# Six PSUM banks for the latent block's tiles, sums of squares two tiles behind the products, inverse roots in place in two alternating places

## The reference, cut to what matters

```python
h = _rmsnorm(h_res, norm_w[l])
proj = h @ w_in[l]
q_lat, kv_lat, k_pe, g_mla, na_q, na_k, na_v, g_na = jnp.split(proj, split_at, axis=-1)
...
q = (_rmsnorm(q_lat, q_lat_w) @ w_uq).reshape(B, L, MLA_HEADS, MLA_NOPE + MLA_ROPE)
kv = (_rmsnorm(kv_lat, kv_lat_w) @ w_ukv).reshape(B, L, MLA_HEADS, MLA_NOPE + MLA_V)
q_nope, q_pe = q[..., :MLA_NOPE], q[..., MLA_NOPE:]
k_nope, v = kv[..., :MLA_NOPE], kv[..., MLA_NOPE:]
q_nope = _rmsnorm(q_nope, qn_w)
k_nope = _rmsnorm(k_nope, kn_w)
...
q_pe = _rope(_rmsnorm(q_pe, qpe_w), cos[None, :, None, :], sin[None, :, None, :])
```

## Time and profile before

| | us |
|---|---|
| median of 3 runs | 1271.04 |
| lowest and highest run | 1270.48, 1272.4 |
| profiled execution | 1273.77 |
| its span in the trace | 1272.1 |
| mean granted TensorE clock | 0.989 |
| latent block on TensorE, first tile to first score matmul | 973.61 to 1060.98 |

### The profile page before, as it was taken

How to read it: one execution, slowest core, us unless ns; L and a number is a source line. 1 busy time by engine, 2 the same in 40 slices (tenths; PEclk the granted TensorE clock), 3 DMA queues, 4 the chain that set the end, 5 groups by cost and what they waited for, 6 DMA issues and landing times.

```text
span 1272.1 us, 18656 instructions
## 1 busy us (share of the span) xinstructions
PE 1195.5 (94%) x7112; PEld 987.8 (78%) x7112; DVE 703.3 (55%) x1170; ACT 544.3 (43%) x1002; POOL 86.2 (7%) x124
## 2 busy tenths in 40 slices
PE   7999999999999998898978899999989788999998
PEld 4665787787788886677955899999979775798467
DVE  3544567676533334779369554445574635455843
ACT  3234321222232223555258554445465556466742
POOL 0002011122100002000000200000000000020500
PEclk9999999999999999899999999999999999999899
DMA  8889355687522232224320345655534332374011
GB/s 304 315 299 323 130 180 164 196 284 248 189 96 100 100 99 66 66 67 133 100 67 1 100 159 174 194 177 188 160 119 145 100 100 66 61 225 138 33 47 53
DMA packets 121366, 183.32 MB, mean 144 GB/s; under 512 B 4305, under 2 KB 92672, under 8 KB 121296
## 3 DMA queue, kind: packets, MB, share of 16 engines
q1 hardware_dynamic: 113744, 154.64, 36.8%
q0 software_dynamic: 7552, 27.73, 6.9%
HBM read 181.31 MB, written 1.05 MB: 143 GB/s over the span
## 4 chain that ended last, share of the span: by engine, by line
PE 80%; DVE 10%; ACT 4%; issue 3%; POOL 1%; DMA 1%; DVEq 0%; SPq 0%; ACTq 0%; POOLq 0%
PE ps L458 19%; PE ps L459 19%; PE ps L460 19%; PE ps L774 2%; PE ps L775 2%; PE ps L776 2%; PE ps L814 2%; DVE wl L443 1%; PE ps L2038 1%; PE ps L2082 1%; ACT wh L436 1%; DVE big L885 1%; PE ps L2369 1%; PE ps L2371 1%; PE ps L2370 1%
## 5 line engine op out<-in xcount | busy, mean ns | idle before, releaser
L443 DVE TENSOR_TENSOR wl<-raw,wh 128x1024 fp32r<-128x1024 f32 (+1 forms) x246 | 296.4, 1209 | 263.3 <-ACT wh L436 260.7
L458 PE MATMUL ps<-hh,wh 128*128 128x256 f32 (+2 forms) x1256 | 420.3, 335 | 17.9 <-DVE hl L588 11.4
L459 PE MATMUL ps<-hl,wh 128*128 128x256 f32 (+2 forms) x1256 | 411.2, 327 | 0.0
L460 PE MATMUL ps<-hh,wl 128*128 128x256 f32 (+2 forms) x1256 | 410.2, 327 | 0.0
L436 ACT ACTIVATE wh<-raw 128x1024 fp32r<-128x1024 f32 (+1 forms) x246 | 252.8, 1031 | 278.1 <-PE ps L460 256.3
L458 PEld LDWEIGHTS ps<-hh,wh 128*128 128x128 f32 x1256 | 238.8, 190 | 60.6 <-issue 27.5
L460 PEld LDWEIGHTS ps<-hh,wl 128*128 128x128 f32 x1256 | 239.2, 190 | 20.9
L459 PEld LDWEIGHTS ps<-hl,wh 128*128 128x128 f32 x1256 | 238.1, 190 | 22.3 <-issue 1.9
L458 PE MATMUL ps<-ah,wh 128*128 128x256 f32 (+2 forms) x392 | 132.5, 338 | 7.4 <-DVE big L870 3.7
L459 PE MATMUL ps<-al,wh 128*128 128x256 f32 (+2 forms) x392 | 129.7, 331 | 0.0
L460 PE MATMUL ps<-ah,wl 128*128 128x256 f32 (+2 forms) x392 | 129.5, 330 | 0.0
(11 more groups left out here) (225 smaller groups left out, 1427.1 us busy)
## 6 DMA issues: line engine op xcount, KB each, us to landing
raw<-in_ffn_w_in SPq DMA_DIRECT2D x44, 1024.0 KB, 5.1
raw<-in_ffn_w_out SPq DMA_DIRECT2D x22, 1024.0 KB, 5.0
raw<-in_w_in SPq DMA_DIRECT2D x22, 1024.0 KB, 5.3
big<-in_w_ada SPq DMA_DIRECT2D x16, 1024.0 KB, 9.3
big<-in_w_ada POOLq DMA_DIRECT2D x24, 512.0 KB, 4.5
ex<-in_w_ada POOLq DMA_DIRECT2D x24, 512.0 KB, 5.2
raw<-in_diff_w_in SPq DMA_DIRECT2D x12, 1024.0 KB, 5.1
raw<-in_w_out SPq DMA_DIRECT2D x8, 1024.0 KB, 4.9
```

The costliest lines, as they stand in the source:

```text
L443: ins = nc.vector.tensor_tensor(place(wl), v, place(wh).bitcast(F32), ALU.subtract)
L458: nc.tensor.matmul(o, w_hi, m_hi, start=first, stop=False, **kw)
L459: nc.tensor.matmul(o, w_hi, m_lo, start=False, stop=False, **kw)
L460: return nc.tensor.matmul(o, w_lo, m_hi, start=False, stop=last, **kw)
```

## The change

In the latent block the tiles take the six banks 0, 1, 2, 5, 6, 7 in turn, and everything behind a head tile's products moves one tile back: the sum of squares of tile i - 2 is issued behind tile i, and so are its inverse root, its scaling (i - 2) and its turning (i - 3). In the other lists the distance stays one tile and the banks 0, 1, 2. Each list now starts at bank 0, and a tile waits for the last user of its bank, across lists. In all lists Ln and Exp work in one place, `rstd[:, h % 2]`, which alternates from head to head, so that ScalarE waits for the scaling of head h - 2 and not of h - 1.

```diff
+        last_in = {}
+        for phase in PHASES:
+            banks = (0, 1, 2, 5, 6, 7) if phase is MLA_UNITS else (0, 1, 2)
+            for i, u in enumerate(phase):
+                u["bank"] = banks[i % len(banks)]
+                u["lag"] = 2 if phase is MLA_UNITS else 1
+                u["prev"] = last_in.get(u["bank"])
+                last_in[u["bank"]] = u
...
-            bank = u["u"] % 3
+            bank = u["bank"]
...
-            if u["u"] >= 3:
-                v = ALL_UNITS[u["u"] - 3]
+            v = u["prev"]
+            if v:
...
-            for i in range(len(phase) + 1):
+            lag = phase[0]["lag"]
+            for i in range(len(phase) + lag):
...
-                if 1 <= i <= len(phase) and phase[i - 1]["kind"] == "head":
-                    u = phase[i - 1]
+                if i >= lag and phase[i - lag]["kind"] == "head":
+                    u = phase[i - lag]
...
-                    positive(act, s_unrm, u["h"])
-                    link(nc.scalar.activation(rstd[0:m, 1, 0:w], ps[0:m, 3 + u["h"] % 2, 0:w], ACT.Ln,
+                    positive(act, s_unrm, u["h"] - 1)
+                    inverse = rstd[0:m, u["h"] % 2, 0:w]
+                    link(nc.scalar.activation(inverse, ps[0:m, 3 + u["h"] % 2, 0:w], ACT.Ln,
                                               bias=eps_c[0:m, 0:1], scale=1.0 / u["dim"]))
-                    nc.scalar.activation(rstd[0:m, 0, 0:w], rstd[0:m, 1, 0:w], ACT.Exp,
-                                         scale=-0.5).then_inc(s_urs, 1)
+                    nc.scalar.activation(inverse, inverse, ACT.Exp, scale=-0.5).then_inc(s_urs, 1)
...
-                            out=dst, in0=o[:, a:b], scalar=par_of(u["gain"])[0:m, :], in1=rstd[0:m, 0, a:b],
+                            out=dst, in0=o[:, a:b], scalar=par_of(u["gain"])[0:m, :], in1=rstd[0:m, u["h"] % 2, a:b],
...
-                if i >= 2 and phase[i - 2].get("rope"):
-                    u = phase[i - 2]
+                if i > lag and phase[i - lag - 1].get("rope"):
+                    u = phase[i - lag - 1]
```

More of the change, by code:

```diff
@@ L842, in units_act @@
                         ins.then_inc(s_ucp, 1)
-                if i >= 1 and phase[i - 1]["kind"] == "head":
-                    u = phase[i - 1]
+                if i >= lag and phase[i - lag]["kind"] == "head":
+                    u = phase[i - lag]
                     m, w = u["cols"], u["w"]
                     act.wait_ge(s_usum, u["h"] + 1)
-                    positive(act, s_unrm, u["h"])
-                    link(nc.scalar.activation(rstd[0:m, 1, 0:w], ps[0:m, 3 + u["h"] % 2, 0:w], ACT.Ln,
+                    positive(act, s_unrm, u["h"] - 1)
+                    inverse = rstd[0:m, u["h"] % 2, 0:w]
+                    link(nc.scalar.activation(inverse, ps[0:m, 3 + u["h"] % 2, 0:w], ACT.Ln,
                                               bias=eps_c[0:m, 0:1], scale=1.0 / u["dim"]))
-                    nc.scalar.activation(rstd[0:m, 0, 0:w], rstd[0:m, 1, 0:w], ACT.Exp,
-                                         scale=-0.5).then_inc(s_urs, 1)
+                    nc.scalar.activation(inverse, inverse, ACT.Exp, scale=-0.5).then_inc(s_urs, 1)
                 for q in halves_after(phase, i):
@@ L855, in units_dve @@
         def units_dve(dve, link, mark, phase):
-            for i in range(len(phase) + 2):
-                if 1 <= i <= len(phase) and phase[i - 1]["kind"] == "head":
-                    u = phase[i - 1]
+            lag = phase[0]["lag"]
+            for i in range(len(phase) + lag + 1):
+                if lag <= i < len(phase) + lag and phase[i - lag]["kind"] == "head":
+                    u = phase[i - lag]
                     m = u["cols"]
```

## The result

The change makes the kernel faster: 1257.89 us (median of 4 runs, 1257.21 to 1258.08) against 1271.32 us (4 runs, 1270.48 to 1272.4) of the kernel before. The ratio is 0.9889, 95% interval 0.9874 to 0.9904, so 12.2 to 16.0 us of gain around 13.4. The forecast was 1257.5. The profiled execution took 1257.90 us, where the forecast for it was about 1260.3.

The account below looks back on a forecast made before the run. TensorE's waits in the latent block were taken as the bound: 19.4 us lost now, 6.2 then, gain 13.2 + 0.3 = 13.5 us from 1271.04, so 1257.5 us; range 1253.5 to 1261.5.

Parts of the forecast that it names:

- The 15 waits go: Latent block: with six banks TensorE's 15 waits for a VectorE scaling, 12.9 us together, go but for a remnant.
- the restart: TensorE in the latent block: each wait loses a further 0.24 or 0.16 us at its restart, 4.2 us in all.
- The split is late next: Second and third quarters' first value tiles: TensorE waits some 2.0 us for VectorE's split at each; cost 4.5 us.
- Sums that wait for a square: Key heads' quarters: two waits of 0.51 and 0.49 us stay, about 0.65 each with restart; cost 1.7 us with late banks.
- a late bank: Key heads' quarters: 0.2 us added to each of the two remaining waits of a sum for its square.
- The roots: Ln and Exp in one place on ScalarE: the wait for the previous head's scaling goes, off TensorE's path; zero gain.
- the row maximum: Start of the attention: it starts 2.53 us behind the first score matmul; rounding and split come earlier, gain 0.3 us.
- The clock: Latent block: one low-clock fall, 1.5 us of work lost, stays; none or two widen the range 1.5 us each side.
- ScalarE's queue takes the banks' part: Latent block: sums wait for squares at about eight rounding places, giving back some 7 us, 1264.5 us; chance 0.10.
- Slower: Latent block: squares' two places and sums' two banks expose the whole chain at 20 heads, 1292 us; chance 0.05.
- Given back: The latent block ends earlier but the slabs are not there, so no change in time; chance 0.04.
- PSUM double-buffering gave no further gain: Skill page's report on a kernel waiting for data; by that rule the time stays at 1271 us.

Follow-up runs that it names:

- halves first: Against the change: in the step behind V2, first two quarters, ScalarE rounds halves before the root and VectorE splits before scaling; 1258.42 us, ratio 0.9889.
- four banks far: Against the change: four banks (0, 1, 2, 5) in place of six, sum still two tiles behind the products; 1269.83 us, ratio 0.9986 to the kernel before.
- three banks far: Against the change: three banks in place of six, sum still two tiles behind the products; 1303.44 us, ratio 1.0253 to the kernel before.

## Why the prediction was right

*The 15 waits go.* Right: none for a scaling is left in the block. My sum had 19.4 us lost before and 6.2 after, 13.2 of gain. The two blocks differ by 14.55, of which 1.7 are the low clock that stood in the block before (1.5 of it in the earlier trace rows) and does not now; that leaves 12.8. One reading was wrong: the sum of tile i - 6 is issued behind tile i - 4, so three tiles lie between it and tile i, and not four. Three of 0.71 us are 2.1, which is about the chain's 2.2, with the sums between them on top; it was enough. In the restart, the 0.08 us for a tile's second matmul is there where the tile has 128 rows (0.20 behind the first), and not at the four waits of V2 with its 16 rows (0.11); that is 0.3 us in all.

*The split is late next.* Right in place and size. I had 4.8 us from V2's end to V0's start (its terms add up to 4.73), it is 4.7. I had TensorE waiting 2.0 us; from 984.92 to 986.96 it is 2.04, shown as 1.70 of idle because the sum's modelled end lies later. That the chain is ScalarE's queue, with Ln and Exp of a1 in it, was only worked out; the experiment with halves first shows it, since taking these two out of the chain cut each wait from 1.7 to 0.9. It also moved the split ahead of a scaling on VectorE, but VectorE had been idle ahead of that split.

*Sums that wait for a square.* I kept two waits of 0.51 and 0.49 and put them at 0.65 with restart; they are 0.58 and 0.61. The 0.2 each for a late bank did not come.

*The roots.* I put them at zero; in the block they are 0.44 to 0.47, from both sides, and in the time nothing that can be told.

*The end of the block.* A term that I didn't have: the last head is scaled one tile later, and the first score matmul waits for it, 1.05 us of idle, where it waited 0.73 for a copy. Against that the row maximum now starts 2.35 us behind it (1044.54 to 1046.89) instead of 2.53, 0.2 where I had 0.3. The two nearly cancel.

*The clock.* I left it at one fall and let none or two widen the range. There was none, in the block. The two traces with three banks and distance one have one fall there (1.7 us of pulses); all eleven traces with more banks have none. This part of the block's gain I had not claimed. What makes the fall is not shown: four banks far wait for scalings nearly as long in all as the kernel before (12.6 and 12.9 us), with longer single waits, and the clock of that kernel stays at 1.00 in the whole block, also in this stretch and behind it:

```profile
1014.00:1016.00 2.00, 0.30 (x3) 0.08 (x1) 1.87 (x6) 1.02 (x2) 0.00 (x0) 1.00 0.00 0
```

*The time.* The median lies 0.4 us from the forecast, and so near a hit is luck in part: the change's second median, on another chip, is 1.6 us above its first (1.0 by the ratios), and the block gave about 1 us more than the 13.5 that I had in all. The profiled execution shows it, 2.4 us below my 1260.3, and its first score matmul at 1044.5 where I had 1047.5; 1.9 us of this are from ahead of the block.

*The rivals.* "ScalarE's queue takes the banks' part" did not happen with distance two, but it is just what six banks at distance one show: 6.3 us of waits for squares. "Slower" named the two places of squares and the two banks of sums as what would set the pace, and they did not: only two sums wait for a square, 1.2 us. Its price, the whole chain exposed at every head, is what three banks far paid by another cause, the bank: I had 21 us and it cost 32, with the clock that I had not counted in it. "Given back": the stretch behind the block is 211.66 us long against 211.12. The sentence of the Trainium skill that "PSUM double-buffering gave no further gain" ("TensorE: Matmul & The Clock Gate", section "HAM oscillation — how this bites in real kernels") is told of a kernel whose loop had already been restructured so that it does more matmuls between its waits for data. It did not carry over: here the wait was for a bank, and one bank more took 12.35 us out of the block.

What I did not foresee is how the gain divides. I wrote of "six banks and two tiles of distance" as one step. By itself the distance makes the kernel 32 us slower, the fourth bank wins 12.35 of the 14.55 us, and the distance wins 1.7 more only with banks beyond the fourth.

## What to carry to other kernels

When an engine waits for a place to come free, count the tiles between the release of the place and its next user, and remember that any step that is moved later uses one of them up: here one more place took away nearly the whole wait, and a longer distance without more places was a loss (30 us of the block with three, 8 with four). When places are there, look at what stands in a helper engine's queue ahead of what the main engine needs next; here two instructions of 0.8 us together in the wrong order cost 0.8 us at each of two places. And judge such small steps by the length of the stretch in the trace, when the time of a whole run varies by more than the step.

## What the runs showed of the hardware

The time of an execution is scattered by more than the small steps above, and the traces show two sources ahead of the block, where all versions are nearly alike. The first is the start: the same matmul comes at 40.1 us in one trace and at 43.5 in another. The second is the clock: from that matmul to the block it takes 929.2 us in the one trace that loses 5.1 us of pulses ahead of the block, 929.8 to 930.1 in the nine that lose 8.5, and 931.1 to 932.1 in the four that lose 13.7. So 8.5 us more of lost pulses cost 2 to 3 us here. Rows of stretches in the change's trace and in its second one:

```profile
640.00:660.00 20.00, 13.88 (x77) 8.53 (x77) 12.41 (x19) 9.30 (x22) 0.00 (x0) 0.91 0.32 105
...
920.00:940.00 20.00, 14.69 (x95) 13.25 (x94) 15.06 (x41) 13.21 (x38) 3.06 (x4) 0.91 0.14 43
```

```profile
640.00:660.00 20.00, 14.80 (x76) 8.76 (x74) 12.11 (x19) 9.30 (x22) 0.00 (x0) 0.83 0.32 105
...
920.00:940.00 20.00, 14.91 (x90) 13.71 (x88) 14.16 (x41) 11.01 (x37) 3.84 (x5) 0.74 0.18 53
```

The same code at the same places is granted 0.91 or 0.83, and 0.91 or 0.74. The clock is not all of the scatter, though: eight of the ten runs of four banks far have the same mean granted clock of 0.989, and their times lie between 1268.33 and 1272.24 us. Two executions of the change reach the block at 971.72 and 974.76 us, 3.0 us apart, and their blocks are 72.82 and 72.83 us long. That is why a step of 1.6 us was clear in the block and not in the median.
